# Two RMS norms in a row, behind the second network, computed as one: weighted squares beside plain ones, one product of both factors, the residual rescaled later

## The reference, cut to what matters

```python
# end of first_block (EPS = 1e-6)
h = h + conv_ffn(rmsnorm(h, f_norm[1]), ...)
x = rmsnorm(h, final_norm)                  # x = h * rsqrt(mean(h*h) + EPS) * final_norm
# start of second_block (NORM_EPS = 1e-5)
hn = _rmsnorm(x, norm_mix_g[0]) * (1 + sc1) + sh1      # goes into x @ s5_w_in
...
x = x + g1 * s5_mixer(hn)                   # the residual is the scaled x, not h
```

## Time and profile before

| | us |
|---|---|
| median of 3 runs | 2829.54 |
| the runs | 2827.99, 2829.54, 2833.63 |
| the profiled execution, its own time | 2834.37 |
| its span in the trace | 2832.4 |
| PE busy in it | 2689.1 (95%) |
| DVE busy in it | 1520.2 (54%) |
| ACT busy in it | 1054.1 (37%) |
| POOL busy in it | 1202.9 (42%) |
| mean granted PE clock | 0.958 |

### The profile page before, as it was taken

The page is one execution under the profiler, slowest core; times in us unless marked ns, Lnnn a source line. Parts: engine busy times, 40 slices in busy tenths (PEclk is TensorE's granted clock), DMA queues, the critical chain, the costliest instruction groups (busy, mean ns, idle before and its releaser), DMA issues.

```text
span 2832.4 us, 36017 instructions
## 1 busy us (share of the span) xinstructions
PE 2689.1 (95%) x13759; PEld 2207.6 (78%) x13759; DVE 1520.2 (54%) x2025; ACT 1054.1 (37%) x1461; POOL 1202.9 (42%) x548
## 2 busy tenths in 40 slices
PE   7998799999989989999978999999999998999998
PEld 6887667888779667888867878888777877788887
DVE  4473357767585656646576555543554654322224
ACT  4543324333333653333332222232245673232222
POOL 3343243444344544444432135454434666444442
PEclk9999889999999999999989999999999998999999
DMA  4323113345423215555348436553223321222322
GB/s 130 105 75 89 45 45 119 112 134 156 123 86 134 75 46 156 186 163 197 122 134 240 125 109 232 187 184 118 93 74 106 116 93 60 90 90 89 104 89 75
DMA packets 365303, 333.12 MB, mean 118 GB/s; under 512 B 40752, under 2 KB 340208, under 8 KB 365040
## 3 DMA queue, kind: packets, MB, share of 16 engines
q1 hardware_dynamic: 331008, 264.03, 30.3%
q10 hardware_dynamic: 34160, 67.22, 6.7%
HBM read 308.56 MB, written 22.64 MB: 117 GB/s over the span
## 4 chain that ended last, share of the span: by engine, by line
PE 76%; DVE 6%; ACT 2%; issue 2%; DMA 1%; POOL 1%; SPq 0%; ACTq 0%; DVEq 0%; POOLq 0%
PE bank L269 20%; PE bank L271 20%; PE bank L270 20%; PE bank L283 3%; PE bank L284 2%; PE bank L288 2%; PE bank L1724 1%; PE bank L1745 1%; PE bank L1733 1%; PE bank L2419 1%; PE bank L2414 1%; PE bank L384 1%; DVE xt L429 1%; DVE sq_x L354 0%; PE bank L912 0%
## 5 line engine op out<-in xcount | busy, mean ns | idle before, releaser
L259 POOL TENSOR_TENSOR w_lo<-w_raw,w_hi 128x1024 fp32r<-128x1024 f32 x384 | 968.2, 2543 | 1319.5 <-ACT w_hi L207 1303.9
L269 PE MATMUL bank<-x_hi,w_hi 128*128 128x512 f32 x1936 | 764.7, 395 | 5.8 <-DVE m_r L2737 1.9
L270 PE MATMUL bank<-x_lo,w_hi 128*128 128x512 f32 x1936 | 757.2, 391 | 0.0
L271 PE MATMUL bank<-x_hi,w_lo 128*128 128x512 f32 x1936 | 756.6, 391 | 0.0
L207 ACT ACTIVATE w_hi<-w_raw 128x2048 fp32r<-128x2048 f32 x206 | 394.2, 1914 | 857.9 <-PE bank L271 770.7
L269 PEld LDWEIGHTS bank<-x_hi,w_hi 128*128 128x128 f32 x1936 | 366.2, 189 | 85.6 <-issue 7.4
L270 PEld LDWEIGHTS bank<-x_lo,w_hi 128*128 128x128 f32 x1936 | 366.0, 189 | 77.2 <-issue 2.2
L271 PEld LDWEIGHTS bank<-x_hi,w_lo 128*128 128x128 f32 x1936 | 365.8, 189 | 76.7
L269 PE MATMUL bank<-m_hi,w_hi 128*128 128x512 f32 x384 | 149.6, 390 | 0.0
L271 PE MATMUL bank<-m_hi,w_lo 128*128 128x512 f32 x384 | 149.4, 389 | 0.0
L270 PE MATMUL bank<-m_lo,w_hi 128*128 128x512 f32 x384 | 149.4, 389 | 0.0
(11 more groups left out here) (479 smaller groups left out, 4488.4 us busy)
## 6 DMA issues: line engine op xcount, KB each, us to landing
w_raw<-in_mlp_w SPq DMA_DIRECT2D x128, 512.0 KB, 4.4
ada_w<-in_ada_w ACTq DMA_DIRECT2D x96, 512.0 KB, 4.9
w_raw<-in_f_w_up SPq DMA_DIRECT2D x88, 512.0 KB, 5.1
w_raw<-in_m_w_in SPq DMA_DIRECT2D x40, 512.0 KB, 4.7
w_raw<-in_a_w_in SPq DMA_DIRECT2D x32, 512.0 KB, 5.0
w_raw<-in_f_w_down SPq DMA_DIRECT2D x32, 512.0 KB, 4.2
w_raw<-in_w_kv SPq DMA_DIRECT2D x16, 512.0 KB, 4.0
w_raw<-in_s_w_glu SPq DMA_DIRECT2D x16, 512.0 KB, 5.3
```

Source lines behind the costliest of these rows:

```text
L259: op = pool.tensor_tensor(w_lo[s][:, part], w_raw[s][:, part], w_hi[s][:, part].bitcast(F32), ALU.subtract)
L269: pe.matmul(dst, hi_l, hi_r, start=start, stop=False)
L270: pe.matmul(dst, hi_l, lo_r, start=False, stop=False)
L271: return pe.matmul(dst, lo_l, hi_r, start=False, stop=stop)
```

## The change

On DVE, the sum of a second set of squares is kept beside the first while the down-projection still runs. ACT makes these squares, of `h * final_norm`, by its own scale operand. When both sums over the features are there, with S the mean of h squared and W the mean of (h * final_norm) squared, the factor of both norms together is rsqrt(W + eps2 * (S + eps1)), and the factor of the first alone rsqrt(S + eps1). Both are spread over a bank by transposes, the one over bank 5, the other over bank 4. The S5 input is made from the unscaled `h` with a merged gain (`mid_gain`) and the factor of both; its temporary tiles lie in PSUM banks 6 and 7 (`MID_X`) and no longer in SBUF. After that DVE rescales `h` in place (`mid_scale_dve`), and PE's first chunk product waits for it, as it overwrites bank 4. A root of a constant (`root_ready`) at the start of the down-projection makes ACT load its table there. ACT's rounding of the last weight slot comes behind its last two weighted squares.

```diff
+        mid_col = sb("mid_col", [P, 7, TT])
+        mid_gain = sb("mid_gain", [P, KD])
...
+        MID_X = (bank[6][:, :], bank[7][:, :])
...
+        def root_ready(act):
+            act.activation(ncol[:, 0, 0:1], eps_col[:, 0:1], ACT.Sqrt)
...
-        def norm_dve(dve, c, lots, g, shift=None, slot=0, root=True, dst=None):
+        def norm_dve(dve, c, lots, g, shift=None, slot=0, root=True, dst=None, turned=None):
+            x2 = turned or (xt[:, 0, :], xt[:, 1, :])
...
-                dve.scalar_tensor_tensor(xt[:, k % 2, :], h[:, k, :], g(k), RSTD, ALU.mult, ALU.mult).then_inc(n_xt, 1)
+                dve.scalar_tensor_tensor(x2[k % 2], h[:, k, :], g(k), RSTD, ALU.mult, ALU.mult).then_inc(n_xt, 1)
...
+        sqw, sqw_sum = at("sqw", 8, [P, 2, T]), at("sqw_sum", 12, [P, T])
+        def add_weighted(dve, k):
+            dve.wait_ge(w_sq, W_SQ + k + 1)
+            dve.wait_ge(mid_done, k + 1)
+            dve.tensor_tensor(sqw_sum[:, :], sqw_sum[:, :], sqw[:, k % 2, :], ALU.add).then_inc(mid_done, 1)
...
                 if c is not None:
                     square(dve, c, i * 2 + o, o, sqs, bank_free, n)
+                if c == 4 and 1 <= i * 2 + o < KD - 1:
+                    add_weighted(dve, i * 2 + o - 1)
...
                 for i in range(4):
                     n = SLOTS[f"f{f}_dn{c}"] + i
+                    if f and c == 2 and i == 0:
+                        root_ready(act)
+                    if f and c == 2 and i == 3:
+                        weighted_act(act, SLOTS["f1_dn2"], i)
                     split_hi(act, n + 2, i % 2, landed(n - i % 2 + 2))
...
+                        if c == 2 and i < 3:
+                            weighted_act(act, SLOTS["f1_dn2"], i)
...
+                if f and c == 2:
+                    dve.memset(sqw_sum[:, :], 0.0).then_inc(mid_done, 1)
...
-        def mid_dve(dve, c, c_next):
-            norm_root(dve, c)
-            squares_start(dve, c_next, SQ_B)
+        M_EPS, M_BOTH, M_OWN, M_RBOTH, M_ROWN = range(5)
+        ROWN = bank[4][:, :]
+        def weighted_act(act, base, i):
+            for k in (2 * i, 2 * i + 1):
+                act.wait_ge(bank_free, 2 * base + k + 1)
+                if k >= 2:
+                    act.wait_ge(mid_done, k)
+                act.activation(sqw[:, k % 2, :], h[:, k, :], ACT.Square, scale=pcol("final_norm", k)).then_inc(w_sq, 1)
+        def mid_pe(pe, c, sqs):
+            def sums(first, src, start, stop):
+                for j in range(TT):
+                    mm = pe.matmul(bank[4][:, first + j:first + j + 1], src[:, j * P:j * P + P], ones[:, 0:1],
+                                   start=(start and j == 0), stop=(stop and j == TT - 1))
+                return mm
+            pe.wait_ge(n_acc, squared(c) + KD)
+            sums(0, sqs[1], True, False)
+            pe.wait_ge(mid_done, KD - 1)
+            sums(TT, sqw_sum, False, False)
+            pe.wait_ge(w_sq, W_SQ + KD - 1)
+            sums(TT, sqw[:, 0, :], False, False)
+            pe.wait_ge(n_sq, KD * c)
+            sums(0, sqs[0][:, 1, :], False, False).then_inc(n_ss, 1)
+            pe.wait_ge(w_sq, W_SQ + KD)
+            sums(TT, sqw[:, 1, :], False, True).then_inc(n_ss, 1)
+            for n, dst, col in ((c, bank[5], M_RBOTH), (c + 1, ROWN, M_ROWN)):
+                pe.wait_ge(n_rcp, n + 1)
+                for j in range(TT):
+                    mm = pe.transpose(dst[:, j * P:j * P + P], mid_col[:, col, j:j + 1].to_broadcast([P, P]), ident[:, :])
+                mm.then_inc(n_bc, 1)
+        def mid_dve(dve, c):
+            dve.wait_ge(mod_done, 3)
+            dve.tensor_tensor(mid_gain[:, :], gain[:, 0, 0:KD], par[:, PAR["final_norm"]:PAR["final_norm"] + KD], ALU.mult).then_inc(mid_done, 1)
+            dve.wait_ge(n_ss, c + 1)
+            dve.tensor_scalar(mid_col[:, M_EPS, :], bank[4][:, 0:TT], EPS2 / D, EPS2 * EPS1, ALU.mult, ALU.add).then_inc(mid_done, 1)
+            dve.wait_ge(mid_done, KD + 1)
+            dve.scalar_tensor_tensor(mid_col[:, M_BOTH, :], bank[4][:, TT:2 * TT], 1.0 / D, mid_col[:, M_EPS, :],
+                                     ALU.mult, ALU.add).then_inc(mid_done, 1)
+            dve.tensor_scalar(mid_col[:, M_OWN, :], bank[4][:, 0:TT], 1.0 / D, EPS1, ALU.mult, ALU.add).then_inc(mid_done, 1)
+            dve.wait_ge(n_std, c + 1)
+            dve.reciprocal(mid_col[:, M_RBOTH, :], mid_col[:, M_RBOTH, :]).then_inc(n_rcp, 1)
+            dve.wait_ge(n_std, c + 2)
+            dve.reciprocal(mid_col[:, M_ROWN, :], mid_col[:, M_ROWN, :]).then_inc(n_rcp, 1)
+            dve.wait_ge(n_bc, c + 1)
+        def mid_act(act, c):
+            for n, src, dst in ((1, M_BOTH, M_RBOTH), (2, M_OWN, M_ROWN)):
+                act.wait_ge(mid_done, KD + 1 + n)
+                act.activation(mid_col[:, dst, :], mid_col[:, src, :], ACT.Sqrt).then_inc(n_std, 1)
+        def mid_scale_dve(dve, c):
+            dve.wait_ge(n_bc, c + 2)
             for k in range(KD):
...
+                dve.scalar_tensor_tensor(h[:, k, :], h[:, k, :], pcol("final_norm", k), ROWN, ALU.mult, ALU.mult).then_inc(mid_done, 1)
...
             slot_half(pe, 0, 0, x_hi, x_lo)
+            pe.wait_ge(mid_done, MID_SCALED)
             s_z_pe(pe, 0)
...
-            norm_pe(pe, 4, SQ_X)
-            norm_pe(pe, 5, SQ_B)
+            mid_pe(pe, 4, SQ_X)
             s5_pe(pe, 5)
...
-            mid_dve(dve, 4, 5)
-            norm_dve(dve, 5, 5, lambda k: gainc(0, k), shift=lambda k: mod[:, 0, k:k + 1], slot=SLOTS["s_in"])
+            mid_dve(dve, 4)
+            norm_dve(dve, 5, 5, lambda k: mid_gain[:, k:k + 1], shift=lambda k: mod[:, 0, k:k + 1], slot=SLOTS["s_in"], root=False, turned=MID_X)
+            mid_scale_dve(dve, 4)
             s5_dve(dve)
```

More of the change, by code:

```diff
@@ L333, in build, with lot_of @@
         RSTD = bank[5][:, :]
+        MID_X = (bank[6][:, :], bank[7][:, :])
         SQ_X = (at("sq_x", 0, [P, 2, T]), at("sq_x_sum", 4, [P, T]))
         SQ_B = (sq, at("sq_sum", 36, [P, T]))
+        def lot_of(c):
+            return c if c < 5 else c - 1
         def squared(c):
-            return TT + KD * (c - 1)
+            return TT + KD * (lot_of(c) - 1)
         def squares_start(dve, c, sqs):
@@ L359, in add_square @@
         def add_square(dve, c, k, o, sqs):
-            dve.wait_ge(n_sq, k + (KD * c - KD + 1))
+            dve.wait_ge(n_sq, k + (KD * lot_of(c) - KD + 1))
             dve.wait_ge(n_acc, k + (squared(c) + 1))
@@ L370, in norm_sums_pe @@
         def norm_sums_pe(pe, c, sqs):
-            pe.wait_ge(n_acc, squared(c + 1))
+            pe.wait_ge(n_acc, squared(c) + KD)
             for j in range(TT):
                 pe.matmul(bank[4][:, j:j + 1], sqs[1][:, j * P:j * P + P], ones[:, 0:1], start=(j == 0), stop=False)
-            pe.wait_ge(n_sq, KD * c)
+            pe.wait_ge(n_sq, KD * lot_of(c))
             for j in range(TT):
@@ L386, in norm_spread_pe, with norm_hi @@
             mm.then_inc(n_bc, 1)
-        def norm_hi(act, lots, slot, shift=None, ks=range(KD), dst=None):
+        def root_ready(act):
+            act.activation(ncol[:, 0, 0:1], eps_col[:, 0:1], ACT.Sqrt)
+        def norm_hi(act, lots, slot, shift=None, ks=range(KD), dst=None, turned=None):
+            x2 = turned or (xt[:, 0, :], xt[:, 1, :])
             dst = x_hi if dst is None else dst
@@ L394, in norm_hi @@
                 if shift is None:
-                    act.activation(dst[:, k, :], xt[:, k % 2, :], ACT.Copy).then_inc(n_hi, 1)
+                    act.activation(dst[:, k, :], x2[k % 2], ACT.Copy).then_inc(n_hi, 1)
                 else:
-                    act.activation(dst[:, k, :], xt[:, k % 2, :], ACT.Identity, bias=shift(k)).then_inc(n_hi, 1)
+                    act.activation(dst[:, k, :], x2[k % 2], ACT.Identity, bias=shift(k)).then_inc(n_hi, 1)
         def norm_act(act, c, eps, lots=0, shift=None, split=True, slot=0):
@@ L420, in low @@
                 if shift is None:
-                    dve.tensor_tensor(d_lo[:, k, :], xt[:, k % 2, :], d_hi[:, k, :].bitcast(F32),
+                    dve.tensor_tensor(d_lo[:, k, :], x2[k % 2], d_hi[:, k, :].bitcast(F32),
                                       ALU.subtract).then_inc(n_lo, 1)
                 else:
-                    dve.scalar_tensor_tensor(d_lo[:, k, :], xt[:, k % 2, :], shift(k), d_hi[:, k, :].bitcast(F32),
+                    dve.scalar_tensor_tensor(d_lo[:, k, :], x2[k % 2], shift(k), d_hi[:, k, :].bitcast(F32),
                                              ALU.add, ALU.subtract).then_inc(n_lo, 1)
@@ L432, in norm_dve @@
             low(KD - 1)
+        mid_done = sem("mid_done")
+        sqw, sqw_sum = at("sqw", 8, [P, 2, T]), at("sqw_sum", 12, [P, T])
[3 more added lines that the diff above has]
+            dve.tensor_tensor(sqw_sum[:, :], sqw_sum[:, :], sqw[:, k % 2, :], ALU.add).then_inc(mid_done, 1)
         def add_h(dve, base, i, s, c, sqs):
@@ L1286, in build @@
         o_n, o_g = sem("o_n"), sem("o_g")
+        w_sq, W_SQ = b_vc, 2 * TT
```

(13 more changed lines are left out.)

## The result

The changed kernel takes 2874.43 us (median of 4 runs, 2872.72 to 2875.22); the kernel before, beside it, 2830.3 us. The ratio is 1.0161 [1.0148, 1.0174], in brackets its 95% interval: 44 us slower, where 9.5 us faster was forecast. The profiled execution took 2874.31 us, with a span of 2872.5.

What follows compares the result with a forecast made beforehand. PE, busy 95% of the span, was taken as the bound, so only stretches where it idles could give much. 8.95 us at the norm plus 0.5 from the clock's return, rounded to 9.5, gave 2820.0 us, range 2815.5 to 2825.5.

Steps and rivals of the forecast that it cites:

- What follows hangs on PE and on chains begun by it, and moves with it: Everything behind the S5 start was taken to keep the local gain, 9.5 us in all.
- Slower: Rival: PSUM tiles ahead of S5 take 3.7 us or more each instead of 1.45; 2837.4 us at 4 us; chance 0.03.
- DVE's lateness: End of the down-projection: added additions make DVE 2.8 us late at the seventh sum, bounds 0 to about 5.2.
- The sign of being wrong: At the norm: sums beginning before 1457.5 or after 1461 would show the forecast wrong; 1458.95 was expected.
- The sums: PE's five batches of column products before the norm, at half clock: 8.8 us, ending at 1467.75.
- Columns, root, reciprocal: Between sums and spread: two DVE column instructions 0.45 us, root 0.26, reciprocal with hand-overs 0.27.
- The four transposes: The norm factor's spread on PE: 0.60 us at full clock, doubled to 1.2 at half clock, plus 0.1 for hand-overs.
- To the first tile: From the down-projection's last wide matmul to the first `xt`: 13.4 us, with `xt` at 1470.0, 8.95 us earlier.
- The clock's return: After the first S5 matmul: full clock returns sooner than the 5.8 us before, gaining 0.5 us, between 0 and 0.9.
- The rescale: DVE's eight instructions on `h` after the tiles: 5.3 us, done at 1487.2, hidden by 14 us before the first chunk product.
- The end: Whole kernel: 2829.54 - 9.5 = 2820.0 us, range 2815.5 to 2825.5.
- The rival of the rising clock: Rival: the clock rises during the sums at the norm, 5.0 us more gained, 2815.0 us; chance 0.06.

Runs made afterwards that it cites:

- filled-up kernel: The changed kernel plus an unused 96-byte tile behind `mid_gain`, making the working area's shift 256 bytes: 2819.24 us against 2826.18 for the kernel before, ratio 0.9975.
- the one without a filler: The changed kernel with `mid_col` and `mid_gain` allocated ahead of `w_raw`, moving weights and working area both by 160 bytes: 2819.33 us against 2829.58 before.

## Why the prediction was wrong

**The step that failed** is the sentence "What follows hangs on PE and on chains begun by it, and moves with it", and that no term stood for where the new tiles lie. The diff shows two tiles allocated ahead of all that PE streams. I followed every instruction and no address: the pitch of the 9720 wide matmuls was taken as fixed, without a reason. It grew by 3.4% at full clock, which cost 0.0186 of the time, 53 us, against a local gain of 7 to 10. None of the rivals had this mechanism. "Slower" had the sign, for another reason: the tiles in PSUM start 1.45 us apart, as before (1468.96 to 1470.41 in the filled-up kernel).

**The local steps** can be judged in the filled-up kernel, whose pitch is that of before. Its timeline:

```profile
1454.07 0.39 PE L274 MATMUL bank<-act_hi,w_lo 128*128 128x512 f32 x1
...
1456.38 1.34 PE L1996 MATMUL bank<-ones,sq_x_sum 128*128 128x1 f32 x8 [1.92 <-DVE sq_x_sum L371]
...
1457.59 1.84 PE L1996 MATMUL bank<-ones,sqw_sum 128*128 128x1 f32 x8
...
1462.71 1.84 PE L1996 MATMUL bank<-ones,sqw 128*128 128x1 f32 x8
...
1464.59 0.16 DVE L2019 TENSOR_SCALAR mid_col<-bank 128x4 f32<-128x4 f32 x1 [6.26 <-PE bank L1996]
...
1465.45 1.97 PE L2012 MATMUL bank<-ident,mid_col 128*128 128x128 f32 x8 [0.90 <-DVE mid_col L2025]
...
1466.61 1.41 DVE L443 SCALAR_TENSOR_TENSOR bank<-h,mid_gain,bank 128x512 f32<-128x512 f32 x2 [1.11 <-PE bank L2012]
...
1468.29 0.77 PE L286 MATMUL bank<-x_hi,w_hi 128*128 128x512 f32 x1 [0.87 <-ACT x_hi L410]
...
1478.37 5.35 DVE L2040 SCALAR_TENSOR_TENSOR h<-h,par,bank 128x512 f32<-128x512 f32 x8
```

- *DVE's lateness:* the sums start 1.9 us after the wide matmuls' end (1454.46), forecast 2.4. Right in kind: additions do wait for POOL (one took 2.88 us at 1450.87).
- *The sign of being wrong* that the sums begin before 1457.5 came up by the letter, with 1456.38 here; the down-projection itself ends 2.1 us earlier in this trace, and to its end the lateness is as forecast. In the changed kernel they begin at 1475.47, far behind the other bound, 1461: that sign was right to fire.
- *The sums:* from 1456.38 to 1464.55, 8.2 us, forecast 8.8. The first batch still had some of the full clock.
- *Columns, root, reciprocal:* 0.9 us to the spread at 1465.45, forecast 0.98. *The four transposes* and the hand-over: 1.16 us, forecast 1.3.
- *To the first tile:* 12.15 us in all, forecast 13.4. To the first S5 matmul 13.8, before 24.1 (1480.66 - 1456.56): 10.3 us gained, forecast 8.95.
- *The clock's return:* 0.5 us were forecast. Full rate comes back 5.96 us after the first S5 matmul, as before (1480.66 to 1486.62). The term is zero here. It is no fixed number: 3.88 us in the changed kernel (1486.72 to 1490.60), 4.28 in the one without a filler.
- *The rescale* ends at 1483.7, the chunk product that waits for it starts at 1498.40: hidden, with 14.7 us of cover (14 forecast). Nothing later was found to give time back.
- *The end:* 2819.24 and 2819.33 us in the two kernels that only mend the place, forecast 2820.0. Against the kernel before on their chips these are 6.9 and 10.3 us less, forecast 9.5; the spread of before's runs (2822.65 to 2829.08 on one chip) is larger than the difference between the two. That the forecast lies within 1 us of both is in part luck, as the kernel before itself took 2826.18 and 2829.58 us on the two chips.

**The rival of the rising clock** falls. From 1477 to 1486 PE was busy in 7.95 of 9.00 us of the changed kernel, and the granted clock stayed at its lower level, 1.2 GHz:

```profile
1477.00:1486.00 9.00, 7.95 (x37) 7.46 (x36) 2.05 (x9) 2.59 (x5) 4.65 (x2) 0.50 1.05 357
```

The rule of the Trainium skill, TensorE: Matmul & The Clock Gate, Part 1, that a sustained busy stretch lifts the clock, would by itself have had it rise here; this stretch of column products and transposes did not bring it.

## What to carry to other kernels

A diff that allocates a tile also moves every tile behind it: before costing its instructions, work out how far apart the loaded weights and the streamed activations then lie, and keep that distance as it was (put small tiles in front of both, or fill up). When a result misses everywhere at once, compare the start-to-start distance of the commonest instruction in a stretch that the change does not touch; 10 us of one window pointed to it here, and the runs with shifted tiles showed it. And a local gain can be judged on its own only after such a common factor is taken out.

## What was not expected of the hardware

Back-to-back 128x512 matmuls, each with its own load of 128x128 weights, start every 226.7 ns at full clock in the unbroken stretches looked at, when the streamed tile lies a multiple of 256 bytes from the weights' tiles, and every 229 to 234.5 ns at the seven other distances tried (steps of 32 bytes), up to 2.0% of the kernel's time. Moving both together by 32, 64 or 160 bytes costs nothing. The pattern is not symmetric, and one pair of shifts gave two pitches in one run. Which access of PE meets which is not shown by these runs.
